# Rounded-weight slots, staged rows and norms handed over piece by piece in a two-block transformer kernel

## The reference

```python
def second_block(x, c, ctx, c_ctx, ...):          # cut
    for l in range(DEPTH):
        hc = rmsnorm(h_ctx, g_pre_mix[l]) * (1.0 + csc1) + csh1      # 256 context tokens
        # last layer: only keys and values are made from hc
        ...  c_attn, c_sgu, c_four, then merge, residual, feed-forward, residual
        hx = rmsnorm(x, g_pre_mix[l]) * (1.0 + sc1) + sh1            # 1024 latent tokens
        px = hx @ w_in[l]
        q, k, v, u, gv, f = jnp.split(px, [Q_END, K_END, V_END, U_END, G_END], axis=-1)
        q, k = rope(q), rope(k)
        attn = latent_window_attention(q, k, v, ck, cv, sink[l])     # 3 blocks of 128 + context
        sgu = spatial_gating(gelu(u), gelu(gv), w_sgu[l], b_sgu[l], g_sgu[l])
        four = fourier_mix(f)                                        # real part of a 2D FFT
        y = merge_heads(attn, sgu, four, g_mix[l], w_out[l])         # 3 rmsnorms, @ w_out
        x = x + g1 * rmsnorm(y, g_post_mix[l])
        hx2 = rmsnorm(x, g_pre_ff[l]) * (1.0 + sc2) + sh2
        x = x + g2 * rmsnorm(squared_relu_mlp(hx2, w_ff1[l], w_ff2[l]), g_post_ff[l])
    return x
```

## Time and profile before

| | |
|---|---|
| median of 3 runs | 4272.48 us (4271.44 to 4273.14) |
| the profiled execution | 4272.9 us, span on the core 4270.7 us |
| busy: PE, DVE, ACT, POOL | 3805.2, 2166.8, 1714.6, 1555.4 us |
| granted TensorE clock, mean | 0.956 of full speed |
| HBM read | 397.32 MB, 95 GB/s over the span |
| loads of a chunk (`wraw<-in_w`) | 544 of 512 KB, 3.5 us from issue to landing |

### The profile page before, as it was taken

The page is one execution under the profiler, slowest core; times in us unless marked ns, Lnnn a source line. Parts: engine busy times, 40 slices in busy tenths (PEclk is TensorE's granted clock), DMA queues, the critical chain, the costliest instruction groups (busy, mean ns, idle before and its releaser), DMA issues. The chain is left out here.

```text
span 4270.7 us, 60415 instructions
## 1 busy us (share of the span) xinstructions
PE 3805.2 (89%) x22828; PEld 3059.4 (72%) x22828; DVE 2166.8 (51%) x2741; ACT 1714.6 (40%) x2935; POOL 1555.4 (36%) x704
## 2 busy tenths in 40 slices
PE   4989999999996798877999788999799779999997
PEld 3867767667665677656788777887677668877886
DVE  5435536445444566657325647325666664347225
ACT  3345345354353444444223334224444453234222
POOL 1433434334332322223444564443322224444443
PEclk8999999999998899988999999999899999999999
DMA  6423424333323221112232443332321122332223
GB/s 236 138 98 123 136 104 143 116 114 124 131 94 103 84 70 50 50 50 78 90 94 93 127 138 100 94 93 85 89 69 50 50 69 86 95 95 89 93 93 108
DMA packets 127195, 421.17 MB, mean 99 GB/s; under 512 B 17408, under 2 KB 19088, under 8 KB 126352
## 3 DMA queue, kind: packets, MB, share of 16 engines
q1 hardware_dynamic: 120080, 407.45, 29.6%
q10 hardware_dynamic: 6912, 10.90, 0.7%
HBM read 397.32 MB, written 6.29 MB: 95 GB/s over the span
## 5 line engine op out<-in xcount | busy, mean ns | idle before, releaser
L1739 POOL TENSOR_TENSOR wlo<-wraw,whi 128x1024 fp32r<-128x1024 f32 x454 | 1097.5, 2423 | 1859.4 <-ACT whi L1753 1858.9
L2453 PE MATMUL lin<-h_hi,whi 128*128 128x512 f32 (+1 forms) x2016 | 764.6, 386 | 107.1 <-DVE h_lo L2127 39.3
L2453 PE MATMUL lin<-h_lo,whi 128*128 128x512 f32 (+1 forms) x2016 | 749.0, 379 | 0.0
L1753 ACT ACTIVATE whi<-wraw 128x1024 fp32r<-128x1024 f32 x454 | 477.3, 1055 | 651.4 <-PE lin L2460 555.5
L2453 PEld LDWEIGHTS lin<-h_hi,whi 128*128 128x128 f32 x2016 | 398.0, 197 | 194.7 <-issue 112.5
L501 POOL TENSOR_TENSOR wlo<-wraw,whi 128x1024 fp32r<-128x1024 f32 x130 | 314.3, 2418 | 586.9 <-ACT whi L596 586.9
L2453 PE MATMUL lin<-a_hi,whi 128*128 128x512 f32 (+1 forms) x1280 | 479.4, 381 | 46.7 <-ACT whi L1753 38.8
L2453 PE MATMUL lin<-a_lo,whi 128*128 128x512 f32 (+1 forms) x1280 | 474.9, 377 | 0.0
L2460 PE MATMUL lin<-h_hi,wlo 128*128 128x512 f32 (+1 forms) x2016 | 461.5, 372 | 4.9 <-POOL wlo L1739 4.9
L2453 PEld LDWEIGHTS lin<-h_lo,whi 128*128 128x128 f32 x2016 | 397.5, 197 | 68.7 <-issue 3.3
L2460 PEld LDWEIGHTS lin<-h_hi,wlo 128*128 128x128 f32 x2016 | 352.0, 189 | 71.5 <-POOL wlo L1739 8.8
(11 more groups left out here) (339 smaller groups left out, 5998.7 us busy)
## 6 DMA issues: line engine op xcount, KB each, us to landing
wraw<-in_w SPq DMA_DIRECT2D x544, 512.0 KB, 3.5
mod_ring<-in_w_ada SPq DMA_DIRECT2D x96, 512.0 KB, 4.6
mod_ring<-in_w_mod SPq DMA_DIRECT2D x32, 512.0 KB, 4.6
wraw<-in_dft_tokens SPq DMA_DIRECT2D x32, 512.0 KB, 3.5
turn<-turn SPq DMA_DIRECT2D x144, 64.0 KB, 2.1
first_ring<-in_w_mod SPq DMA_DIRECT2D x16, 512.0 KB, 17.1
tmp<-tmp SPq DMA_DIRECT2D x80, 64.0 KB, 2.0
x<-in_x ACTq DMA_DIRECT2D x2, 2048.0 KB, 21.1
```

Source lines behind the costliest of these rows:

```text
L1739: nc.gpsimd.tensor_tensor(wlo[:, s, 0:D], wraw[:, s, 0:D], whi[:, s, 0:D].bitcast(F32), ALU.subtract)\
L1753: nc.scalar.activation(whi[:, s, 0:D], wraw[:, s, 0:D], ACT.Copy).then_inc(*w_hi.one)
L2453: nc.tensor.matmul(bank[s][:, 0:p.w], whi[:, s, k * P:(k + 1) * P], h[:, k, 0:p.w], start=(k == 0 and h is parts[0]), stop=False)
```

## The change

- **Weight slots.** A new semaphore `hi_used` is set by TensorE at the last matmul that reads `whi` of a chunk. `split_high` waits for it (of two chunks before) in place of `lin_done`, and stands earlier in ACT's order, ahead of squares, attention's copies and evacuations (`refill`). `split_low` on GpSimd now waits for `lin_done` of two chunks before as well. Both also in the first block.
- **By blocks.** Chunk 0 of a projection or merge row, and the last chunk of a row whose successor has a norm ready, run piece by piece with all three products (`by_blocks`), behind a wait for the whole `w_split`. With `end`, TensorE sets `h_used` after each piece, so that `high` and then `low` of the next norm overwrite `h_hi` and `h_lo` piece by piece. Fourier steps 14 and 15 have the like (`last_blocks`).
- **Attention's copies first.** DVE does `turned(i-1, 0)` and `normalize` ahead of additions (and behind scales); ACT does `exponentials`, then `refill` or roots, then `turned`, then squares.
- **Places of norms.** In merges squares go to k = 1 (2), k = 2 (2) and k = 4 (4), sums and roots to k = 5, scales to k ≥ 6, lows to k = 7 ahead of the post addition. In the Fourier phase squares to h = 9 and 10, sums and roots to h = 11, scales to h = 12 to 14, lows to h = 14 and 15.
- **Two norms in row 0** of layer 0: the context's (squares s = 2 to 5, sum s = 6, scales s = 7 and 8) and row 1's (squares s = 5 to 8 summed in `y`, sum s = 9, scaled in the context's row, s = 3 to 6). In layer 1 row 0 scales row 1's norm at s = 10 and 11. Sums come behind the high products.
- **Values.** V2's copy frees `lin` at once; the transposed values go through `bankO`.
- **Feed-forward.** The updates of the row before go from one a chunk (from j = 1) to two a chunk at j = 4 to 7, its sum from behind the first chunk to behind the fourth.

```diff
             def split_low(g, s):
 
                 pool.wait_ge(*w_hi.after(g, 1))
+                pool.wait_ge(*lin_done.after(g, -1))
...
             def split_high(g, s):
 
+                act.wait_ge(*hi_used.after(g, -1))
                 act.wait_ge(*chunk_in[s].after(g, 0))
...
-            def high(kind, n, k):
+            def high(kind, n, k, end=None, last=None):
 
                 sig, w = norms[kind], n.rows.w
                 act.wait_ge(*sig["scaled"].after(n.no, k + 1))
+                if end is not None:
+                    act.wait_ge(*(h_used.after(end, k + 1) if k < KB - 1 else lin_done.after(last, 1)))
...
             # ACT, merge
                 for k in range(KB):
                     i, s = merge_point(l, b, k), k % 2
-                    if nxt and k == 6:
+                    exponentials(l, i)
+                    if nxt and k == 5:
                         mix_roots(nxt)
-                    if ff and k == 5:
-                        root_pre(ff, turnT[0])
-                    attend(l, i)
-                    if nxt and 2 <= k < 6:
-                        for j in MIX_SQUARES[2 * k - 4:2 * k - 2]:
+                    if k < KB - 1:
+                        refill(g + k)
+                    turned(l, i - 1, 0)
+                    if nxt:
+                        for j in merge_squares(k):
                             mix_square(nxt, j)
...
+                    if k == KB - 1:
+                        for j in range(KB - 1):
+                            high(kind, following, j, end_of(l, "merge", b), g + k)
+                        refill(g + k)
+                        high(kind, following, KB - 1, end_of(l, "merge", b), g + k)
                     act.wait_ge(*lin_done.after(g + k, 1))
...
             def hidden(gi, grp, j, s, w):
 
+                split_high(gi + 2, s)
                 act.wait_ge(*lin_done.after(gi, 1))
                 act.wait_ge(*a_ready.after(grp, j - 1))
                 nc.scalar.activation(tmp[:, 4 + s, 0:w], bank[s][:, 0:w], ACT.Relu).then_inc(*lin_free.one)
-                split_high(gi + 2, s)
...
             # DVE, project
+                        for n, first, ps in sums_beside(l, p.b):
+                            for k in squares_at(first, s):
+                                add_square("pre", n, k, pre_sums(n))
+                            if n.rows.context or l:
+                                for k in scales_at(first, s):
+                                    scale("pre", n, k)
+                        if l == 0 and p.context and 3 <= s < 7:
+                            for k in (2 * s - 6, 2 * s - 5):
+                                scale("pre", nxt, k)
+                        if attending:
+                            turned(l, s - 1, 0)
+                            normalize(l, s)
+                            turned(l, s - 1, 1)
+                if nxt:
                     for k in range(KB):
-                        low("pre", n, k)
+                        low("pre", nxt, k)
...
             # DVE, feed_forward
                 for j in range(FF_CH):
                     hidden(g0 + j, p.ff_no * FF_GROUPS, j, j % 2, p.w)
-                    if j:
-                        update(prev, j - 1)
-                update(prev, KB - 1)
+                    if j >= 4:
+                        update(prev, 2 * j - 8)
+                        update(prev, 2 * j - 7)
...
             # PE
+            def by_blocks(g, s, p, when=None, end=None):
+
+                pe.wait_ge(*lin_free.after(g, 1))
+                pe.wait_ge(*w_hi.after(g, 1))
+                pe.wait_ge(*w_split.after(g, 1))
+                for k in range(KB):
+                    if when:
+                        pe.wait_ge(*when(k))
+                    for n, (w, h) in enumerate(((whi, h_hi), (whi, h_lo), (wlo, h_hi))):
+                        last = nc.tensor.matmul(bank[s][:, 0:p.w], w[:, s, k * P:(k + 1) * P], h[:, k, 0:p.w],
+                                                start=(k == n == 0), stop=(k == KB - 1 and n == 2))
+                        if k == KB - 1 and n:
+                            last.then_inc(*(hi_used if n == 1 else lin_done).one)
+                    if end is not None and k < KB - 1:
+                        last.then_inc(*h_used.one)
```

More of the change, by code:

```diff
@@ L767, in evacuate, with refill @@
                         act.sem_inc(gate_ready.sem, 1)
-                split_high(it, s + 2)
+            def refill(it, s):
+                if s not in (GV, RV):
+                    for c in range(s + 1 if s in (GV + 1, RV + 1) else s + 2, s + 3):
+                        split_high(it, c)
             def mod_rows(it, s):
@@ L1121, in high_products @@
                     for h in (h_hi, h_lo):
-                        nc.tensor.matmul(bank[c % 2], whi[:, c % 2, k * P:(k + 1) * P], h[:, k, :],
-                                         start=(k == 0 and h is h_hi), stop=False)
+                        last = nc.tensor.matmul(bank[c % 2], whi[:, c % 2, k * P:(k + 1) * P], h[:, k, :],
+                                                start=(k == 0 and h is h_hi), stop=False)
+                last.then_inc(*hi_used.one)
             def low_products(it, c):
@@ L1146, in token_half @@
                                                     start=(k == n == 0), stop=(k == KB - 1 and n == 2))
-                if half:
-                    last.then_inc(lin_done.sem, 2)
+                    if half and n:
+                        last.then_inc((hi_used if n == 1 else lin_done).sem, 2)
             def out_products(it, c, ks):
@@ L1522, in second_block @@
         w_hi, w_split = (Sig(t[n].sem, 1, before) for n in ("w_hi", "w_split"))
-        lin_done, lin_free = (Sig(t[n].sem, 1, before) for n in ("lin_done", "lin_free"))
+        lin_done, lin_free, hi_used = (Sig(t[n].sem, 1, before) for n in ("lin_done", "lin_free", "hi_used"))
         EVACUATED = 3
@@ L1647, in next_in, with sums_beside, squares_at, end_of @@
             at = order.index(b)
-            return pre_mix(l, order[at + 1]) if at + 1 < len(order) and not (l and b == NB) else None
+            return pre_mix(l, order[at + 1]) if at + 1 < len(order) else None
+        def sums_beside(l, b):
+            if b == 0:
+                return [(pre_mix(l, NB), 2, bankO), (pre_mix(l, 1), 5, bankT)] if l == 0 else [(pre_mix(l, 1), 5, bankO)]
+            return []
+        def squares_at(first, s):
+            return {0: (0, 1), 1: (2, 3), 2: (4, 5), 3: (6, 7)}.get(s - first, ())
+        def end_of(l, stage, b=None):
+            ends = [("in", 0), ("in", NB), ("dft", None), ("merge", 0), ("merge", 1), ("merge", NB),
+                    ("in2", NB), ("in2", 0), ("dft2", None), ("merge2", 0), ("merge2", 1)]
+            return ends.index((stage + ("2" if l else ""), b))
         def next_ff(l, b):
@@ L1677, in merge_point, with merge_squares, mix_bank, scales_at @@
             return MERGE_POINT + MERGE_ROWS[l].index(b) * KB + k
+        def merge_squares(k):
+            return {1: MIX_SQUARES[0:2], 2: MIX_SQUARES[2:4], 4: MIX_SQUARES[4:8]}.get(k, ())
+        def mix_bank(n, part):
+            if part < 2:
+                return turnT[part]
+            return turnT[0] if n.rows.l == 0 and n.rows.b == 1 else bankO
+        def scales_at(first, s):
+            return range(4 * (s - first - 5), 4 * (s - first - 4)) if 5 <= s - first < 7 else ()
         @block.sync
@@ L1902, in project @@
             def project(l, p):
-                n, nxt, attending = pre_mix(l, p.b), next_in(l, p.b), p.b == 1
-                if p.in_no and not (l and p.context):
-                    for k in range(KB):
-                        high("pre", n, k)
-                for s in range(2 if l and p.context else IN2):
+                nxt, attending, last = next_in(l, p.b), p.b == 1, 1 if l and p.context else IN2 - 1
+                for s in range(last + 1):
                     if l and p.b == 0 and s == 0:
@@ L2452, in high_products @@
                     for h in parts:
[L2453 to L2454 removed]
+                        last = nc.tensor.matmul(bank[s][:, 0:p.w], whi[:, s, k * P:(k + 1) * P], h[:, k, 0:p.w],
+                                                start=(k == 0 and h is parts[0]), stop=False)
+                if ks[-1] == KB - 1:
+                    last.then_inc(*hi_used.one)
             def low_products(g, s, p, parts):
@@ L2576, in token_half @@
                                                     start=(k == 0 and h is h_hi and not low), stop=(k == KB - 1 and low))
-                if half and low:
-                    last.then_inc(lin_done.sem, 2)
+                if half:
+                    last.then_inc((lin_done if low else hi_used).sem, 2)
             def turn_values(p):
-                pe.wait_ge(*v_raw.after(p.in_no, 1))
+                pe.wait_ge(*lin_free.after(p.in_at + V2, EVACUATED))
                 for n in range(p.tiles):
                     tile = slice(n * P, (n + 1) * P)
```

(7 more changed lines are left out.)

403 lines of the change are left out of this document (219 added, 184 removed).

## The result

The changed kernel takes 4242.01 us (median of 4, 4238.54 to 4247.0) against 4271.96 in the same comparison, a ratio of 0.9935 (95% interval 0.9919 to 0.9950). So it is faster, by 30 us, where 83 were forecast. Its profiled execution has a span of 4241.0 us, 29.7 less than before, at a mean granted clock of 0.956 as before. The time is inside the stated range of 4128 to 4260, but the gain is about a third of the forecast one: the sum is off by 54 us, and the rest of this text is about where these 54 are.

A forecast was written before the change was run, and what follows sets the result against it. The prediction took TensorE, busy 89% of the span, as the bound, with gains only from its idle stretches and clock. Terms summed to −83.5 us against 4272.9 profiled: 4189.4, or 4189.0 as a median, range 4128 to 4260.

The forecast's parts named there:

- Feed-forward, 512 wide: Earlier split_high saves 0.85 us at each of 16 group starts, doubled updates give back 3: −11 (−16 to +2).
- Feed-forward, context: Context row's feed-forward: two chunks take 7.2 us, ended by the DMA, which the change doesn't move: 0 (−4 to +4).
- First block: First block: four waits of 0.9 us for whi go, −3.5; with wlo's new wait −8 to +5.
- Projections, layer 0: Layer 0's projections: row 0 +14 for preparing two norms, context row −22; sum −8 us (−30 to +8).
- lock step: Row 0's roped chunks, 7.3 us apart before, wait on rotation, scales, additions and squares; chunks 7 and 8 take 10.9.
- Projections, layer 1: Layer 1's projections: sum behind 16 matmuls, scales at s = 10 and 11, row starts earlier: −10 us (−16 to 0).
- Fourier phase: Fourier steps: attention's copies and normalize first remove idle time, −16.5 us a layer, −33 in all (−50 to −5).
- Merge of row 0: Row 0's merges beside attention: additions held by GpSimd's wlo, +6 in layer 0, −3 in layer 1: +3 (−12 to +25).
- rival (C): Slower by the lock: wlo released by lin_done holds VectorE's ops; 2.42 us on 48 of 64 chunks, +116: 4305; chance 0.09.
- Other merges: Merges without attention: piecewise lows shorten waits for h_lo, context −8, row 1 of layer 1 −13: −21 us (−35 to −5).
- Handover: Piecewise passing of lows at k = 7 of row 0's merges: void in layer 0, −6 us in layer 1.
- rival (D): Handovers keep their waits, as the next norm's high stands behind a copy waiting for TensorE: 4231; chance within the forecast's 0.66.

The follow-up runs named there:

- e10_ff_late: Changed kernel, but in feed-forward's hidden chunks ACT rounds the next weights behind relu again, as before the change: 4260.13 us.
- e1_swap: Changed kernel, but in merges VectorE takes the second half of attention's copies, turned(i-1, 1), before the post addition: 4210.36 us, ratio to before 0.9861.
- e4_late_refill: Changed kernel, but in merges ACT rounds the next weights after the evacuation, as before the change: 4199.95 us, ratio to before 0.9836.
- e5: Changed kernel, but GpSimd's split_low in the second block subtracts 512 of the 1024 columns, leaving part of the computation out: 4113.14 us.

## Why the prediction was wrong in size, step by step

- **Feed-forward, 512 wide: right, slightly low.** −15.2 by stage, −11 forecast. The 16 starts kept 0.3 us, not 0.4, so they gave 16, and e10_ff_late, which takes back only this order, loses 17.7. The rows gained 15.2, so the doubled updates and the rest cost about 1 to 2.5 us where +3 was booked.
- **Feed-forward, context: right in the sum, in part by luck.** +2.2, for 0 (−4 to +4). Load, `whi` and `wlo` set its time, and halving `wlo` took 40 us off it. But the +2.2 hide two terms of which the prediction has none: its first eight chunks take 3.6 us less and the rest 5.8 more (228.5 to 234.3). With relu ahead of `whi` again (e10_ff_late) the rest takes 234.1, so that order isn't the cause; it stays open.
- **First block:** −6.6 for −3.5, near the lower bound of −8. Not taken apart.
- **Projections, layer 0: right.** −7.7 against −8, and by its parts: row 0 +10.6 (+14), context −17.2 (−22), the lock step 9.9 us apart (10.9 worked out, as four scales took 1.67 and not 2.4).
- **Projections, layer 1:** −4.3 against −10. TensorE waits less for `h_lo`, but still 2.6 for the sum and 3.6 for the gate's values in row 0: the lock step, which I had let cost nothing more here. The eight scales without the last two are also 7.1 of the 9.51 us, not the 8 that I took.
- **Fourier phase:** −26 against −33, in range. Steps 1 to 8 gave 3.7 of 4.5 in layer 0, and 9 to 15 gave 8.5 where 12 were booked.
- **Merge of row 0: this step failed.** Booked were +3 for both layers, measured are +15.8 and +16.3. It had the right mechanism and the right direction: the additions are held, and 6 of the 11 additions of layer 0's row 0 take 2.3 to 2.7 us where all had 0.7. But it said that a third of this ends on TensorE's path in layer 0 (+6), and 3 us in layer 1. Measured, the values wait 2.2 to 3.7 us in most of row 0's chunks with attention, where they waited 0.7 to 1.7, so most of it ends there. The stage is 2 us a chunk longer, which is the prediction's own sign of failing (worse than 1). I had not asked what is queued behind the waiting addition on its engine: it is `turned(i-1, 1)`, the copy that the values of the same step wait for. The rival (C), which prices exactly that, I argued away because the copies read PSUM and are not held; they are not held, but they stand in line. With the copy taken out of that line (e1_swap) 33.4 us come back in three merges, and with `wlo` late 42.6 (e4_late_refill), so (C) was right in kind, not on 48 chunks but on the 14 with attention, and some of the 42.6 are its sequels in sums, lows and clock. The prediction had also put ACT's `split_high` ahead of attention's copies at nothing; the two runs leave at most 9.2 us for it, and no run tests it alone.
- **Other merges:** −2.4 against −21. Row 1's in layer 0, which has no term in the sum although three of its chunks carry attention, is +9.2; e4 takes 9.9 back. The context's −1.8 for −8: the wait for `h_lo` at its end fell only from 8.5 to 5.7. That updates keep VectorE late, as the prediction said, no run tests. Row 1 in layer 1, −9.8 for −13, worked: the wait ahead of feed-forward fell from 5.19 to 1.54 us.
- **Handover:** it was expected to be void in layer 0's merges with attention, and to bring −6 at the end of row 0's merge in layer 1. These 6 did not come: even with `wlo` late (e4_late_refill) that stage is 2.3 us longer than before. Scales and lows end 8 us after the last product, and the sum of the finished row waits behind them. So rival (D) was right at this place, by another cause than it named.

With GpSimd's instruction halved, VectorE's additions as a group go from 1037 to 791 ns, while attention's copies out of PSUM (128x384) take 0.54 to 0.56 us, every one, in the kernel before, the changed one and e5 (group of the changed kernel, then of e5):

```profile
L2167 DVE TENSOR_TENSOR tmp<-tmp 128x512 f32<-128x512 f32 (+1 forms) x151 | 156.6, 1037 | 112.8 <-ACT tmp L1809 107.7
```
```profile
L2167 DVE TENSOR_TENSOR tmp<-tmp 128x512 f32<-128x512 f32 (+1 forms) x151 | 119.4, 791 | 111.6 <-ACT tmp L1809 106.6
```

With the exclusive lock of the Trainium skill ("SBUF — State Buffer", "Who interferes with whom") this trace agrees for instructions on two SBUF tiles: an addition of 512 columns takes 0.68 us alone and up to 2.9 us beside GpSimd. They are not the only ones that stretch. `normalize`, which reads one tile and a column of factors, has a median of 0.55 us and a longest of 2.65.

## What to carry to other kernels

When an edit moves an instruction of an engine that can hold up another, list what the other engine has queued at that moment, and what stands behind the first of it: the price is not the stretched instruction but all that waits in line behind it. A buffer freed earlier is no gain where nobody waited for it. In the three merges that grew TensorE never waited for `whi` before the change, so the early `whi` only moved `wlo` to a worse time. Such a change is worth making stage by stage: here in feed-forward, where it is worth 18 us, and not in merges, where leaving it out gives back 42.

## What was not expected of the hardware

Halving GpSimd's subtraction (2454 to 1335 ns, for half of the columns) made both kernels 3% faster, though GpSimd is busy for 36 or 37% of the span: 40 us in the context's feed-forward, where it is a link of the cycle that reloads a slot, and the rest in nearly all other stages of the second block. How much of that rest came through VectorE, and how much through chunks that wait for `wlo` itself, is not shown. In feed-forward the holding shows plainly in the means by form (groups of VectorE's instructions, first before and then after). The earlier `whi` moved it from one instruction to its neighbour: in e10_ff_late, with the old place, the two are at 786 and 2350 ns again.

```profile
L2341 DVE TENSOR_TENSOR a_lo<-tmp,a_hi 128x512 f32 x64 | 145.5, 2273 | 62.3 <-ACT a_hi L2025 62.3
...
L2338 DVE TENSOR_TENSOR tmp<-tmp 128x512 f32<-128x512 f32 x128 | 92.8, 725 | 213.3 <-ACT tmp L2021 212.6
```
```profile
L2403 DVE TENSOR_TENSOR tmp<-tmp 128x512 f32<-128x512 f32 x128 | 270.2, 2111 | 298.6 <-ACT tmp L2087 297.7
...
L2406 DVE TENSOR_TENSOR a_lo<-tmp,a_hi 128x512 f32 x64 | 44.3, 693 | 10.3 <-DVE tmp L2403 10.3
```
